# Up projections of an encoder's MLP by seven products of quarters instead of eight

## The reference, cut to what matters

```
h = rms_norm(x, ffn_pre_g[i])                          # (512, 1024)
mlp = square(relu(h @ w_up[i])) @ w_down[i]            # w_up (1024, 4096), w_down (4096, 1024)
x = x + rms_norm(mlp, ffn_post_g[i])
```

## Time and profile before

| | us |
|---|---|
| median of 3 runs | 1919.48 |
| the three runs | 1918.28, 1922.35, 1919.48 |
| the profiled execution | 1917.97 |
| its span in the trace | 1916.3 |
| PE busy | 1879.9 (98%) |
| DVE busy | 1004.1 (52%) |
| ACT busy | 726.2 (38%) |
| POOL busy | 218.0 (11%) |

### The profile page before, as it was taken

How to read it: one execution, slowest core, us unless ns; L and a number is a source line. 1 busy time by engine, 2 the same in 40 slices (tenths; PEclk the granted TensorE clock), 3 DMA queues, 4 the chain that set the end, 5 groups by cost and what they waited for, 6 DMA issues and landing times.

```text
span 1916.3 us, 25723 instructions
## 1 busy us (share of the span) xinstructions
PE 1879.9 (98%) x9898; PEld 1565.9 (82%) x9898; DVE 1004.1 (52%) x1465; ACT 726.2 (38%) x1275; POOL 218.0 (11%) x207
## 2 busy tenths in 40 slices
PE   9999999999999999999999999999999999999997
PEld 7785578889888888897889788897888898888887
DVE  6957955544644343666652356525464274333444
ACT  5226855334423141542123511235553362232232
POOL 0430001000430000103420033200200000000001
PEclk9999999999999999999999999999999999999999
DMA  4330014403232322322332122311351223222321
GB/s 165 119 99 22 1 55 151 135 12 99 68 120 80 106 88 88 108 73 85 99 108 68 34 88 88 112 53 60 119 163 56 66 67 121 88 88 88 113 77 63
DMA packets 86755, 167.51 MB, mean 87 GB/s; under 512 B 5632, under 2 KB 7808, under 8 KB 86400
## 3 DMA queue, kind: packets, MB, share of 16 engines
q1 hardware_dynamic: 86656, 166.15, 26.7%
HBM read 164.03 MB, written 2.10 MB: 87 GB/s over the span
## 4 chain that ended last, share of the span: by engine, by line
PE 88%; DVE 6%; ACT 3%; issue 2%; DMA 0%; SPq 0%; ACTq 0%; DVEq 0%
PE ps L1628 70%; PE ps L1661 6%; DVE half L1090 2%; PE ps L1754 2%; PE ps L1949 1%; DVE w_lo L1043 1%; PE ps L1941 1%; PE ps L1815 1%; PE ps L1879 1%; PE ps L1809 1%; PE ps L1888 1%; DVE small L1308 1%; PE ps L1894 1%; ACT w_hi L617 1%; PE ps L1875 1%
## 5 line engine op out<-in xcount | busy, mean ns | idle before, releaser
L1043 DVE TENSOR_TENSOR w_lo<-raw,w_hi 128x1024 fp32r<-128x1024 f32 x304 | 389.0, 1305 | 304.9 <-ACT w_hi L617 303.3
L617 ACT ACTIVATE w_hi<-raw 128x1024 fp32r<-128x1024 f32 x304 | 314.0, 1056 | 484.2 <-PE ps L1628 478.6
L1628 PE MATMUL ps<-act_hi,w_lo 128*128 128x512 f32 x1244 | 490.2, 394 | 6.6 <-DVE w_lo L1043 4.2
L1628 PE MATMUL ps<-act_lo,w_hi 128*128 128x512 f32 x1248 | 485.8, 390 | 0.0
L1628 PE MATMUL ps<-act_hi,w_hi 128*128 128x512 f32 x1244 | 485.0, 390 | 0.0
L1628 PEld LDWEIGHTS ps<-act_hi,w_lo 128*128 128x128 f32 x1244 | 233.9, 188 | 60.3 <-DVE w_lo L1043 6.3
L1628 PEld LDWEIGHTS ps<-act_lo,w_hi 128*128 128x128 f32 x1248 | 234.8, 188 | 49.9 <-issue 1.9
L1628 PEld LDWEIGHTS ps<-act_hi,w_hi 128*128 128x128 f32 x1244 | 233.8, 188 | 49.2
L1628 PE MATMUL ps<-ff_hi,w_lo 128*128 128x512 f32 x448 | 176.5, 394 | 0.0
L1628 PE MATMUL ps<-ff_lo,w_hi 128*128 128x512 f32 x448 | 176.5, 394 | 0.0
L1628 PE MATMUL ps<-ff_hi,w_hi 128*128 128x512 f32 x448 | 176.5, 394 | 0.0
(11 more groups left out here) (211 smaller groups left out, 2749.6 us busy)
## 6 DMA issues: line engine op xcount, KB each, us to landing
raw<-in_db_w_qkv SPq DMA_DIRECT2D x72, 512.0 KB, 3.7
raw<-in_w_up SPq DMA_DIRECT2D x64, 512.0 KB, 3.7
raw<-in_w_down SPq DMA_DIRECT2D x64, 512.0 KB, 4.0
raw<-in_xa_wkv SPq DMA_DIRECT2D x32, 512.0 KB, 3.7
raw<-in_da_w_qkv SPq DMA_DIRECT2D x24, 512.0 KB, 3.8
raw<-in_xa_wq SPq DMA_DIRECT2D x16, 512.0 KB, 4.5
raw<-in_xa_wo SPq DMA_DIRECT2D x16, 512.0 KB, 3.9
raw<-in_da_w_o SPq DMA_DIRECT2D x8, 512.0 KB, 4.1
```

The source lines that it names most:

```text
L617: nc.scalar.activation(w_hi[:, g % 4], raw[:, g % 4], ACT.Copy).then_inc(w_hi_ready, 1)
L1043: nc.vector.tensor_tensor(w_lo[:, g % 4], raw[:, g % 4], w_hi[:, g % 4].bitcast(f32), ALU.subtract).then_inc(w_lo_ready, 1)
L1628: last = nc.tensor.matmul(ps[:, s + m, 0:width], left, right, start=(k == 0 and n == 0 and not early), stop=(k == KT - 1 and n == 2))
```

## The change

The first chunk stays as it is. The up projections of chunks two to four are made by Strassen's scheme over 2 x 2 quarters. A *block* is 256 weight columns x 1024 features against all 512 tokens. Its weights are cut in four quarters of 512 features x 128 columns (W11, W21 from the upper half, W12, W22 from the lower), the input in four quarters of 512 features x 256 tokens (upper/lower features, front/back tokens). Seven products of 512 features, 128 columns and 256 tokens replace eight. A mixed unit is two blocks (512 columns); there are 6 mixed units, 12 blocks, per layer. Counting from the loads, PE's order in a layer is: up, up, down, down (chunk 1); mixed, mixed, down, down; mixed, mixed, down, down; mixed, mixed, down, down. So blocks come in three runs of four.

The work of a block: POOL makes four sums of quarters from `raw`, of which three go to `sq` and one is made in place; ACT copies seven operands of 128 x 512 to `w_hi` slots and DVE makes the seven remainders; PE does 12 matmuls of 256 tokens per product; ACT and DVE combine the banks; ACT applies relu and square and splits two hidden tiles at once. Bank 0 takes products 1 and 5, bank 2 products 3 and 6, bank 3 products 4 and 7, so DVE must have read bank 2 before product 6 starts.

The input: gain and 1/rms are folded in first (`folded_base_and_rests`, `folded_heads`, `folded_rests`), during the first chunk's two down units; the split of three quarters goes back to `act_hi/lo`, the four sums of input quarters are split into new tiles `t_hi/lo`. The masks are built earlier on POOL. The angle tables of layer 1 move from the last up unit to the down unit before the last.

The diff, cut to its core:

```diff
+P_A11, P_T2, P_T1, P_T3, P_A21, P_A22, P_T4 = range(PRODUCTS)
+BANK_OF = (0, 1, 2, 3, 0, 2, 3)
+SUM_OF = {P_T2: 2, P_T1: 1, P_T3: 4, P_A22: 3}
...
+        def mixed_source(b, i):
+            upper, lower = quarters(2 * (b % 2)), quarters(2 * (b % 2) + 1)
+            return (upper[:, :, 0:P], s2_sb, s1_sb, upper[:, :, P:2 * P], lower[:, :, 0:P], s4_sb, lower[:, :, P:2 * P])[i]
...
 SP
+            def block_read(b, j, ii):
+                sp.wait_ge(mixed_lo, of_block(b, PRODUCTS, PRODUCTS if j % 2 else P_T3 + 1, ii))
...
 POOL
+            def mixed_sums(layer, n, ii=0):
+                for s in range(2):
...
+                    pool.wait_ge(mixed_loaded[2 * s], loads)
+                    pool.wait_ge(mixed_loaded[2 * s + 1], loads)
+                    if b > 0:
+                        pool.wait_ge(mixed_lo, of_block(b - 1, PRODUCTS, P_A22 + 1, ii))
+                    nc.gpsimd.tensor_tensor(s1_sb, w21, w22, ALU.add).then_inc(mixed_sum, 1)
+                    pool.wait_ge(mixed_sum, of_block(b, SUMS, 1, ii))
+                    nc.gpsimd.tensor_tensor(s2_sb, s1_sb, w11, ALU.subtract).then_inc(mixed_sum, 1)
+                    pool.wait_ge(mixed_sum, of_block(b, SUMS, 2, ii))
+                    nc.gpsimd.tensor_tensor(s4_sb, w12, s2_sb, ALU.subtract).then_inc(mixed_sum, 1)
+                    nc.gpsimd.tensor_tensor(w21, w11, w21, ALU.subtract).then_inc(mixed_sum, 1)
...
+                pool.wait_ge(folded_lo, FOLDED * (layer + 1))
+                mixed_sums(layer, 0)
...
 ACT
+            def mixed_head(b, i, ii=0, after_unit=None):
+                if i in SUM_OF:
+                    act.wait_ge(mixed_sum, of_block(b, SUMS, SUM_OF[i], ii))
...
+                    act.wait_ge(product_done, of_block(b - 1, PRODUCTS, i + 1, ii))
...
+                nc.scalar.activation(slot(w_hi, i), mixed_source(b, i), ACT.Copy).then_inc(mixed_hi, 1)
+            def hidden_squares(b, layer, ii=0):
+                act.wait_ge(product_joined, of_block(b, JOINS, JOINS, ii))
+                nc.scalar.activation(hidden_sb[:, S // 2:2 * S], hidden_sb[:, S // 2:2 * S], ACT.Relu).then_inc(hidden_relu, 1)
...
+                nc.scalar.activation(stage_row, hidden_sb, ACT.Square).then_inc(staged, 2)
...
+                nc.scalar.activation(ff_hi[:, m:m + 2, :], stage[:, :, :], ACT.Copy).then_inc(hi_ready, 2)
+            def mixed_block(b, layer, ii=0, next_unit=None, follows=True):
+                for i in range(PRODUCTS):
+                    if i in (P_A11, P_A21):
+                        act.wait_ge(product_done, of_block(b, PRODUCTS, i + 1, ii))
+                    if i == P_A11:
...
+                        nc.scalar.activation(first_sb, bank, ACT.Copy).then_inc(first_read, 1)
+                    if i == P_A21:
+                        act.wait_ge(staged, ii * KT + (STAGED[f"ff{layer}"] + n))
+                        nc.scalar.activation(hidden_sb[:, 0:S // 2], bank, ACT.Relu).then_inc(first_read, 1)
+                    if next_unit is None:
+                        mixed_head(b + 1, i, ii)
+                    elif i in (1, 3):
+                        heads_of(4 * next_unit + i // 2, ii, mixed=b)
+                    if i == P_T2 and follows:
+                        hidden_squares(b - 1, layer, ii)
...
+                def folded_heads(j):
+                    if j == 0:
+                        act.wait_ge(bank_done, 4 * (u + 1) + 4)
+                        act.wait_ge(folded_base, KT * (layer + 1))
+                        for rows, cols in INPUT_QUARTERS:
+                            nc.scalar.activation(act_hi[:, rows, cols], sq[:, rows, cols], ACT.Copy).then_inc(folded_hi, 1)
+                    if j == 1:
+                        for n, (rows, cols) in enumerate(SUM_QUARTERS):
+                            act.wait_ge(folded_sum, 4 * layer + n + 1)
+                            nc.scalar.activation(t_hi[:, n], sq[:, rows, cols], ACT.Copy).then_inc(folded_hi, 1)
...
+                unit(u + 2, None, between=folded_heads)
+                unit(u + 3, None, next_block=b)
+                mixed_block(b, layer, follows=False)
+                mixed_block(b + 1, layer)
+                with act.Fori(0, CHUNKS - 2) as c:
+                    mixed_block(b + 2, layer, c)
+                    mixed_block(b + 3, layer, c, next_unit=u + 4)
+                    unit(u + 4, None, c, after=b + 3)
+                    unit(u + 5, None, c, next_block=b + 4)
+                    mixed_block(b + 4, layer, c, follows=False)
+                    mixed_block(b + 5, layer, c)
...
 DVE
+            def mixed_block(b, layer, ii=0, next_unit=None, follows=True):
+                for i in range(PRODUCTS):
+                    if i == 0:
+                        mixed_rest(b, PRODUCTS - 1, ii)
+                    if i in (P_T2, P_T3, P_T4):
+                        dve.wait_ge(product_done, of_block(b, PRODUCTS, i + 1, ii))
+                    if i == P_T2:
...
+                        nc.vector.tensor_tensor(u2, first_sb, banks[1], ALU.add).then_inc(product_joined, 1)
+                    if i == P_T3:
...
+                        nc.vector.tensor_tensor(u3, u2, banks[3], ALU.add).then_inc(product_joined, 1)
...
+                        dve.wait_ge(staged, ii * KT + (STAGED[f"ff{layer}"] + first_tile(b)))
+                        nc.vector.tensor_tensor(hidden_sb[:, 3 * S // 2:2 * S], u3, banks[2],
+                                                ALU.add).then_inc(product_joined, 1)
+                    if i == P_T4:
+                        nc.vector.tensor_tensor(hidden_sb[:, S // 2:3 * S // 2].rearrange("p (n s) -> p n s", n=2),
+                                                u2.rearrange("p (n s) -> p n s", n=1).broadcast_to([P, 2, S // 2]),
+                                                ps[:, 4 * (b % 2) + 2:4 * (b % 2) + 4, 0:S // 2],
+                                                ALU.add).then_inc(product_joined, 1)
+                    if next_unit is None and i >= 1:
+                        mixed_rest(b + 1, i - 1, ii)
+                    elif next_unit is not None and i in (2, 4):
+                        rests_of(4 * next_unit + i // 2 - 1, ii)
+                    if i == P_A21 and follows:
+                        hidden_rests(b - 1, layer, ii)
...
+                def folded_base_and_rests(j):
+                    if j == 0:
+                        for k in range(KT):
+                            nc.vector.scalar_tensor_tensor(sq[:, k, :], x_sb[:, k, :], gcol(layer, "ffn_pre_g", k), rstd[:, :],
+                                                           ALU.mult, ALU.mult).then_inc(folded_base, 1)
+                    if j == 1:
+                        for n, (rows, cols) in enumerate(INPUT_QUARTERS):
+                            dve.wait_ge(folded_hi, FOLDED * layer + n + 1)
+                            nc.vector.tensor_tensor(act_lo[:, rows, cols], sq[:, rows, cols], act_hi[:, rows, cols].bitcast(f32),
+                                                    ALU.subtract).then_inc(folded_lo, 1)
...
+                        for n, (dst, left, right) in enumerate(((a11, a12, a11), (a12, a22, a12), (a22, a22, a11), (a21, a21, a22))):
+                            dve.wait_ge(folded_sum, 4 * layer + n)
+                            nc.vector.tensor_tensor(dst, left, right, ALU.subtract).then_inc(folded_sum, 1)
...
 PE
+            def mixed_unit(layer, n, ii=0, after_units=None):
...
+                    for i in range(PRODUCTS):
+                        pe.wait_ge(mixed_lo, of_block(b, PRODUCTS, i + 1, ii))
+                        if i == P_A21:
+                            pe.wait_ge(first_read, of_block(b, FIRSTS, 1, ii))
+                        if i == P_A22:
+                            pe.wait_ge(product_joined, of_block(b, JOINS, 3, ii))
...
+                        for t in range(HALF):
+                            for p, (left, right) in enumerate(((wl, hi), (wh, lo), (wh, hi))):
+                                last = nc.tensor.matmul(bank, left[:, t, :], right[:, t, :], ...)
+                        last.then_inc(product_done, 1)
```

More of the change, by code:

```diff
@@ L1050, in unit @@
+            def unit(u, bank=None, ii=0, between=None, done=2, ahead=2, second=2, first_steps=None, next_block=None):
                 for j in range(2):
@@ L1055, in unit @@
                 for m in range(5):
-                    if m == 0 and u + 1 < TOTAL_UNITS:
+                    if m == 0 and next_block is not None:
+                        for i in range(PRODUCTS - 1):
+                            mixed_rest(next_block, i, ii)
+                    elif m == 0 and u + 1 < TOTAL_UNITS:
                         rests_of(4 * u + 4, ii)
@@ L1562, in _ @@
+                b += 2 * MIXED_UNITS - 2
+                v = u + 2 * CHUNKS
+                mixed_block(b, layer)
+                mixed_block(b + 1, layer, next_unit=v)
+                unit(v, share_of(v, 0), between=angles_between(1) if layer == 0 else None)
+                v += 1
```

(2 more changed lines are left out.)

260 lines of the change are left out of this document (205 added, 55 removed).

## The result

| | before | after |
|---|---|---|
| median, us | 1918.88 (4 runs) | 1943.12 (4 runs, 1941.85 to 1944.94) |
| ratio to before | 1 | 1.0124, 95% interval 1.0106 to 1.0141 |
| profiled execution, us | 1917.97 | 1944.32 |
| its span, us | 1916.3 | 1942.5 |
| PE busy, us | 1879.9 | 1873.1 |

The change costs 24.2 us. The forecast was 1931, a cost of 12, so it has the sign and half of the size; the time lies inside its range of 1911 to 1948.

The account below looks back on a forecast made before the run. The prediction took TensorE (PE), busy 98% of the span, to bound the kernel. Its terms, -26.0 + 19.2 + 19.4 = +12.6 us, gave 1930.6 on the profiled execution, 1932 on the median, stated as 1931; range 1911 to 1948.

Parts of the forecast that it names:

- term 1: Up chunks two to four: seven eighths of PE's columns at 0.1167 us per 256-column matmul, -26.0 us.
- term 2: Runs of four blocks: PE stops before product six in second and third block, 3.2 us per run, +19.2 us.
- term 3: Fold in the first chunk's down units: PE waits 3.4 and 6.1 us per layer, +19.4 us with refilling.
- The rival with steps of 0.125: Blocks: 256-column matmuls take 0.125 us among changing weights, 2.8 us more per run; 1942 us, chance 0.08.
- The last link: Before product six, second block: DVE's s2 remainder, u3, quarter come last, 1.0 us late; ACT's squares, at 7.2, just hidden.
- The shared access: Blocks: DVE remainders and POOL sums, both reading two SBUF tensors, exclude each other, each handing the other its whole duration.
- The rival in which it does not bind (1922): Blocks: the port rule does not bind, stalls of 1.7 us per run; 1922 us, chance 0.10.
- the one nearly without stops (1911): Blocks: s2 copy, remainder and joins get through before product six, nearly no stalls; 1911 us, chance 0.11.
- The rival of sums of 2.0 us: Blocks: POOL's quarter sums take 2.0 us, 2.1 us more in two blocks per run; 1956 us, chance 0.12.
- the forecast's step that POOL starts later there: Third block: ACT, held at s2, ran late, so POOL starts at 2.7 instead of 2.0; quarter 1.9 us late.

Follow-up runs that it names:

- e8: Changed kernel with the weights ahead of the fold (e1) and both reorderings on ACT and DVE (e4): 1895.29 us, ratio 0.9877 to the kernel before.
- e5: Changed kernel with 8 or 16 unread matmuls added on PE in the wait before product six of second and third blocks: 1936.53 us.
- e2: Changed kernel with ACT's relu and square of the previous block issued ahead of the copy of the next block's second weight sum: 1929.51 us.
- e3: Changed kernel with DVE's remainder of the next block's second weight sum issued behind u3 and the quarter: 1941.52 us.
- e4: Changed kernel with both reorderings, ACT's squares first (e2) and DVE's quarter first (e3): 1915.40 us, ratio 0.9975 to the kernel before.
- e9: Changed kernel with POOL's sums cut to one element, each followed by clearing 768 free elements, so POOL is busy but hardly reads: 1924.38 us.
- e6: Changed kernel with POOL's four sums per block made over one element instead of 512, orders and waits unchanged: 1914.97 us.
- e1: Changed kernel with the first down unit's last two weight pairs and the next unit's first two issued ahead of the fold on ACT and DVE: 1929.35 us.
- e11: The kernel of e8 with a second buffer for s4 as well: 1904.83 us, ratio 0.9918 to the kernel before.

## Why the prediction was right in sign and half in size

| step | forecast | measured | from |
|---|---|---|---|
| term 1, fewer columns | -26.0 | -27.2 | e8: 39.01 against 43.54, six times |
| term 2, stops in the blocks | +19.2 | +31.0 | six runs, 265.1 less 6 x 39.01 |
| term 3, the fold | +19.4 | +21.9 | 10.4 and 11.4 us |
| sum | +12.6 | +25.7 | spans: +26.2 |

**Term 1 held.** Steps of 256 columns are 0.114 to 0.119 us in the blocks, as they were in the earlier trace rows; a product is 1.39 us, not 1.40. The rival with steps of 0.125 is gone.

**Term 2 is the step that failed, in size.** Place, pattern and origin were right: second and third block, none in the first and fourth, at product six, behind the quarter, from POOL's late and stretched sums. In the changed kernel's order, forecast stops of 1.0, 1.9 and 0.3 for refilling (3.2 per run) came out as 1.5 and 2.3 in the first run, 1.1 and 2.4 in the second (a block's time less 9.76, and less 1.5 of clock in the third): 3.5 to 3.8. That is 2 to 4 us over six runs. The larger part is a cost that the sum did not have: the half clock behind the third block, 1.5 us per run by e5, 9 in all. The earlier trace rows could not show it, as PE never stopped for 2 us inside the MLP; the one fall of the clock that the trace of before did hold ahead of its last 7 us, 3.4 us near the kernel's start, was not asked about.

**The last link was misread.** "The quarter also waits for the squares of the block before ... just hidden" was the sentence to doubt. It gave that branch 7.2 against the 7.57 at which the quarter was to start, under 0.4 us of cover, and it rested on an s2 copy seen at 5.3 that came at 5.8, since both sums before it were stretched (1.70 and 1.82, not 1.29). ACT's squares ended at 7.7 and the quarter began 0.1 later; DVE's own branch was through at 7.4. e2, e3 and e4 show that the two branches end 0.3 us apart in the second block and 1.2 in the third, so that to cut the later one alone gives half (e2), to cut the other alone nothing (e3), and to cut both everything.

**The shared access** was the forecast's reason for the sums being late. It is at most 20 of 28 us (e9), by the estimate there about 15: hardly more than half, with the plain length of the sums as the rest. The rival in which it does not bind (1922) and the one nearly without stops (1911) ended 21 and 32 us too low; e6 shows that the orders of ACT and DVE alone would have left no stop at all. The rival of sums of 2.0 us did not come: they take 1.4 to 1.6 on average, stretched by meeting DVE, not by their shape: one that meets no remainder takes 1.29 (e1, at 561.28).

**Term 3 held in its chain:** PE resumed at 541.62 and 553.40 where 541.5 and 553.2 were worked out. But the first down unit now began 0.8 us later (522.10), and the chain did not move with it: DVE's remainder of the third pair started at 529.79, 7.7 us behind the unit's start and not 8.4 as in the earlier trace rows. So the stops are 8.9 us (31.30 to the resumption, against 22.40), not 9.7; 1.5 us more went at half clock behind them, which makes the 10.4 of layer 0. In layer 1 half clock lasts 6.8 us at the second stop and takes 2.5 (granted clock 0.91 against 0.94), which makes 11.4. That the whole term came out only 2.5 us too low has some luck in it: 1.6 us of stops too many stood against 4 us of half clock that it did not have.

**What the sum lacked.** It is 13.1 us short, and the half clock behind the stops, which no term had, is 13 of them: 9 in the blocks and 4 in the folds. The other misses cancel (1.2 too little saved by term 1, 1.6 too much stop in term 3, 2.8 too little in term 2).

What stays open: what makes the third block's stop the longer one. The trace agrees with the forecast's step that POOL starts later there (2.45 us into the block, against 1.58), but the reason given for it, that ACT was held, was not taken apart by any run. Open too is whether the last 1.6 to 1.8 us in each layer's first run need POOL's sums ahead of the fold's last splits; that was not tried, and starting POOL sooner by the second buffer made that stop longer (e11).

## What to carry to other kernels

Work taken off the busiest engine is worth its price only if the orders of the others are written anew for it: the same instructions cost 24 us or save 24 us here, by where the weights of three pairs, the squares and one remainder stand in two queues. Where a wait has two branches that end within a microsecond of each other, price both as late, and test them together as well as one by one. And add to each stop of TensorE what it does to the clock behind it: here 1.5 us behind a stop of 2.3.

## What was not expected of the hardware

- Behind 27 of the 28 stops of PE of 1.97 to 2.9 us in blocks, over all these traces, 3.4 us at 0.5 of the clock (1.2 GHz) followed or had begun; across it products six and seven of the changed kernel's third block, 24 matmuls of 256 columns, take 4.45 us instead of 2.8. Behind the stops of 0.6 to 1.7 us in the blocks there was none. It is not a fixed rule in these runs: the 2.56 us stop in the fold had one behind it in 10 of 16 cases, in layer 0 of the changed kernel but not of e4. There PE came sooner to the next wait, which grew from 4.38 to 5.92 us: half clock ahead of a wait that another engine ends costs nothing.
- The clock also fell without such a stop: near 96 us in all traces but that of e3, 8 to 10 us behind a stop of 0.96 us, and between 950 and 975 us in seven of the eleven experiments, with no stop over 0.1 us in the 15 us before it.
- A POOL sum and DVE's remainders lengthen each other (1.41 to 1.72 us on average for 1.29, 862 to 1074 ns for 686), but a POOL operation that only writes leaves DVE's remainders at 686.
- Giving an engine a buffer more, so that it starts up to 3 us sooner, made the kernel 8 us slower than the same kernel without it, where in another order it had made it 18 us faster.
